# A decoder layer with a sparse mixture of experts on one core: expert weights in 2 MB transfers, and a front end split around its row transposes

## The chip, the cores and the metric

The kernel is one program on 1 core of one Trainium2 chip. Its time is the device time of one execution, in microseconds (us), launch to end. Five engines work side by side: TensorE (PE in the profile; PEld is its weight load), VectorE (DVE), ScalarE (ACT), GpSimd (POOL) and SyncE (SP), which here issues nearly all DMA transfers. Sixteen DMA engines share every transfer. "MB" of an expert transfer below is 1,048,576 bytes; the GB/s of the profile are 1e9 bytes per second.

## What is computed

One layer of a decoder for 256 prompt rows and 8 x 4 sample rows, with all weights and caches in float32. A modulation (`silu(c) @ w_ada + b_ada`), an RMS norm, and one wide projection `w_in` feed a sparse attention (compressed, selected and window branch) and a gated recurrence; their merged result goes through `w_out`. Then comes the mixture of experts, in which most of the time is spent:

```python
def moe_ffn(h, w_router, b_router, w_up, b_up, w_down, b_down):
    logits = (xt @ w_router + b_router).astype(jnp.float32)
    top_v, top_i = lax.top_k(logits, TOP_K)          # 4 of 32
    wts = jax.nn.softmax(top_v, axis=-1)
    ...
    for e in range(N_EXPERTS):
        z = xt @ w_up[e] + b_up[e]                   # 1024 x 2048
        gate = jnp.minimum(z[:, :D_EXPERT], SWIGLU_LIMIT)
        up = jnp.clip(z[:, D_EXPERT:], -SWIGLU_LIMIT, SWIGLU_LIMIT)
        act = (up + 1.0) * gate * jax.nn.sigmoid(SWIGLU_ALPHA * gate)
        out = out + gate_dense[:, e:e + 1] * (act @ w_down[e] + b_down[e])   # 1024 x 1024
```

The compressed branch needs a convolution of the cached keys and values (`compress`: blocks of 32 rows, stride 16, against `cmp_w1`).

## The kernel before

All tiles lie in one SBUF array, `arena`; PSUM is eight banks. Each engine has its own hand-written program, and semaphores join them; nothing is scheduled by a planner in the parts that follow, except the order of some steps in the middle of the program, which is not touched.

**Front end.** TensorE first transposes the gathered cache rows (L764). Then it runs `convolve(0)` (L786: 32 taps by two halves, 64 matrix products of 504 columns, two records each in the trace), then for each of three row tiles `rows_to_hT(n)` (L753: transposes of the input rows) followed by `modulation(n)` (L798: one slab of `w_ada` against the conditioning vectors), then `position_terms` (L774, L778), `modulation` 3 to 5, four transposes (L815), `convolve(1)`, and the compressed keys and values (L821, L824).

**Slabs.** `w_ada` (12 slabs) and the main part of `w_in` (7 slabs) come in slabs of 2 MB (the last one smaller) with runs of 2 KB, in the order of `SLABS`: six of `w_ada`, one of `w_in`, then turns of both. Three buffers hold them; SP issues slab i (L570) as soon as slab i-3 is used (`slab_used`). A slab of `w_in` costs TensorE the products at L1002, L1003 and L1008. Behind slab 9 SP issues `state_win`, the cached rows of the window, for six of the eight samples in one transfer of 3 MB (L594), once both convolutions are done (`pre_ps`). `window_keys` reads it after the slabs.

**Experts.** Tokens are packed into chunks of 64 slots; 34 chunks serve the 32 experts, so two experts have two chunks. An expert's weights come in 12 pieces of 1 MB: eight of `w_up` (128 rows each, a run of 8 KB in a partition) and four of `w_down` (256 rows, two neighbouring rows in a partition, also 8 KB). The pieces go round a ring of 21 places. For each chunk TensorE adds the bias (L1320), multiplies pieces q = 0 to 7 (L1328, eight records a piece), dispatches the next chunk's tokens (L1299), transposes the activations (L1343, L1305), and multiplies pieces q = 8 to 11 (L1358, eight records a piece). It waits for a piece by `ld_piece`, and counts it used by `piece_used`. SP refills a place when the piece in it is used for the last time: for an expert with two chunks that is in the second one, since the wait (L710 for the last, L705 for the others) counts from `until`, the number of that expert's last chunk. Before the first chunk SP fills the ring in steps: 8 pieces once the merged rows are there (`mT`), 4 after the output projection (`out_ps`), 8 after `y1`, `h2` and the router (`lg_ps`), the last one after `wdiag`.

**End.** GpSimd scatters each chunk's result to `slots` in DRAM (L2302, L2303). After the last one SP reads them back in two transfers of 2 MB with runs of 16 KB (L719), and TensorE sums them (L1382).

Of the kernel before, what the change touches and what calls it, by code (L numbers as in the profile page):

```python
# [243 lines left out]
ORDER = (2, 0, 1)  # L244
PIECES = 12 * E


def build(nc, A, O):

    with ExitStack() as ctx:  # L250
# [166 lines left out]
        def ftake(n, *shape):  # L417
# [83 lines left out]

        up_pairs = up.rearrange("p (m t v) -> p m v t", m=2, v=2)
        in_chunk = [view(low + 12 * NCHUNK * i, 12 * NCHUNK, 12, NCHUNK) for i in range(2)]
# [11 lines left out]
        assert ring_at - routed >= 2 * D and ring_at + 7 * 2 * D <= wo_at and CONSTS["chunk0"][0] + NCHUNK <= x_at - 2 * D  # L515
        places = ([ring_at + 2 * D * i for i in range(7)] + [x_at - 2 * D] + [ring_at + 2 * D * i for i in range(7, 16)]
                  + [x_at, spare, spare + 2 * D, routed])
        ring = [view(a, 2 * D) for a in places]
        R_ = len(ring)
# [29 lines left out]
        def _(sp):  # L549
# [33 lines left out]
            for i in range(3, len(SLABS)):  # L583
                load_slab(i)
                if i == 6:
                    sp.wait_ge(S("pair_ps"), 32)
                    for w, name in enumerate(("norm_mix_post", "norm_ffn_pre", "norm_ffn_post")):
                        for j in range(4):
                            src = A[name][0].rearrange("(n j c) -> j n c", j=4, c=P)[j]
                            sp.dma_start(wn[32 * j:32 * j + 32, 2 * w:2 * w + 2], src.unsqueeze(0).broadcast_to([32, 2, P])  # L590
                                         ).then_inc(S("ld_wn"), 16)
                if i == 9:
                    sp.wait_ge(S("pre_ps"), 2)
                    sp.dma_start(arena[:, gates_at:gates_at + 6 * 1024].rearrange("p (b c) -> p b c", b=6),  # L594
                                 A["state_win"][0, 0:6].rearrange("b (p s) k g d -> p b (s k g d)", s=4)).then_inc(S("ld_win"), 16)
            sp.wait_ge(S("mod_v"), 12)
# [87 lines left out]
            for n in range(R_):  # L684
                if n == 8:
                    sp.wait_ge(S("out_ps"), 5)
                if n == 12:
                    sp.wait_ge(S("y1"), 3)
                    sp.dma_start(xd[0:TP].rearrange("(i p) d -> p i d", p=P), x[:, 0:2]).then_inc(S("st_state"), 16)
                    sp.dma_start(xd[TP:TP + NS], x[0:NS, 2]).then_inc(S("st_state"), 16)  # L690
                    sp.wait_ge(S("h2"), 3)
                    for r in range(4):
                        sp.dma_start(bias[32 * r:32 * r + E], A["b_up"][0][:, 512 * r:512 * r + 512]).then_inc(S("ld_bias"), 16)
                    sp.wait_ge(S("lg_ps"), 3)
                if n == 17:
                    sp.wait_ge(S("st_state"), 64)
                if n == R_ - 1:
                    after(sp, "wdiag")
                load_piece(n)
            after(sp, "tab")  # L700
            for n in range(R_, PIECES):
                e, q = (n - R_) // 12, (n - R_) % 12
# [28 lines left out]
        def _(pe):  # L731
# [48 lines left out]

            def convolve(g):
                for s in range(32):
# [4 lines left out]
                last.then_inc(S("pre_ps"), 1)  # L787

# [27 lines left out]
            last.then_inc(S("modT_ps"), 1)  # L816
            convolve(1)
            pe.wait_ge(S("gelu"), 4)
# [86 lines left out]
            def window_keys(b):  # L905
                pe.wait_ge(S("ld_win" if b < 6 else "ld_win2"), 16)
                bank = to_ring("win", b)
# [395 lines left out]
            def chunk_T():  # L1303
                for k in range(4):
                    last = nc.tensor.transpose(banks[2][:, P * k:P * k + P], xr[:, P * k:P * k + P], ident)  # L1305
                last.then_inc(S("xcT_ps"), 1)
# [7 lines left out]
            for e in range(E):  # L1314
                before = pe.value_load(tab[0:1, E + e:E + e + 1], min_val=0, max_val=CMAX)
                upto = pe.value_load(tab[0:1, e:e + 1], min_val=1, max_val=CMAX)
                with pe.Fori(before, upto) as c:
# [5 lines left out]
                    for q in range(8):  # L1323
                        n = 12 * e + q
                        pe.wait_ge(S(f"ld_piece{n % R_}"), 16 * (n // R_) + 16)
                        for part in range(2):
                            for s in range(2):
                                last = mm(banks[part][SLOT * s:SLOT * s + SLOT, :], xcT[:, q],  # L1328
                                          ring[n % R_][:, D * part + 512 * s:D * part + 512 * s + 512], start=False, stop=q == 7)
                        last.then_inc(S("piece_used"), 1)  # L1330
# [11 lines left out]
                    for k in range(4):  # L1342
                        last = nc.tensor.transpose(banks[(3, 6)[k // 2]][:, P * (k % 2):P * (k % 2) + P], up_pairs[:, k // 2, k % 2], ident)  # L1343
                        if k % 2:
                            last.then_inc(S("aT_ps"), 1)
# [3 lines left out]
                    for q in range(8, 12):  # L1349
                        n = 12 * e + q  # L1350
                        if q < 10:
                            pe.wait_ge(S("aT"), c * 2 + (q - 7))
                        pe.wait_ge(S(f"ld_piece{n % R_}"), 16 * (n // R_) + 16)
                        for v in range(2):
                            f = 2 * (q - 8) + v
                            lhs = aT[:, P * (f % 4) + SLOT * (f // 4):P * (f % 4) + SLOT * (f // 4) + SLOT]
                            for s in range(2):
                                last = mm(banks[4][SLOT * s:SLOT * s + SLOT, :], lhs,  # L1358
                                          ring[n % R_][:, D * v + 512 * s:D * v + 512 * s + 512], start=f == 0, stop=f == 7)
                        last.then_inc(S("piece_used"), 1)  # L1360
# [972 lines left out]
```

## Time and profile before

| | us |
|---|---|
| median of 3 runs | 1562.64 (1561.87 to 1564.94) |
| the profiled execution's own time | 1568.19 |
| its span, first to last instruction | 1565.0 |
| PE busy in the span | 1431.4 (91%) |
| DVE busy | 362.5 (23%) |
| ACT busy | 296.9 (19%) |
| POOL busy | 81.4 (5%) |
| data moved | 513.19 MB, mean 328 GB/s |

A share of busy time says little here, since the stages have different limits: the span has a front end (0 to about 265 us), a middle (to about 515 us), the ring's filling with the router (to about 580 us), the experts (to about 1531 us) and an end. Which wait ends last must be read in each. In a timeline row the bracket at the end is the engine's idle time just before and what ended it.

### The profile page before, as it was taken

How to read it: one execution, taken by the hardware profiler on the slowest of the kernel's cores; microseconds unless marked ns; L12 is line 12 of the kernel's file. 1: busy time of each engine (PE TensorE's matmuls, PEld its weight loads, DVE VectorE, ACT ScalarE, POOL GpSimd, SP SyncE). 2: the span in 40 equal slices, each digit the busy share in tenths (PEclk: the TensorE clock that was granted, in tenths of full speed). 3: DMA queues.
4: the chain of work that ended last, by engine and by line, in shares of the span. 5: the costliest groups of instructions: out<-in, count | busy, mean ns of one | idle time of the engine just before them, and what ended most of it. 6: DMA issues, size and time to landing. Idle time of an engine off the chain costs nothing.

```text
span 1565.0 us, 21038 instructions
## 1 busy us (share of the span) xinstructions
PE 1431.4 (91%) x8523; PEld 632.6 (40%) x8523; DVE 362.5 (23%) x833; ACT 296.9 (19%) x568; POOL 81.4 (5%) x108
## 2 busy tenths in 40 slices
PE   4999999979998979999999999999998998899895
PEld 4564455456766443333333333333332322232231
DVE  5220012347752351111111111121211111111123
ACT  4110003455420221101111111111110110111011
POOL 2000001300000000000000000000000000000000
PEclk9899999989899969999999999999999999999998
DMA  9791775414177589979999999999999999999994
GB/s 277 239 334 54 271 255 183 130 43 153 50 199 261 217 358 402 419 293 421 420 420 420 420 420 419 421 421 419 421 420 420 420 420 420 420 420 420 420 403 173
DMA packets 119925, 513.19 MB, mean 328 GB/s; under 512 B 12945, under 2 KB 42025, under 8 KB 68194
## 3 DMA queue, kind: packets, MB, share of 16 engines
q1 hardware_dynamic: 113090, 489.91, 79.3%
q0 software_dynamic: 6752, 22.06, 4.1%
q8 instruction: 66, 1.08, 0.3%
q14 instruction: 17, 0.14, 0.0%
HBM read 501.06 MB, written 19.22 MB: 332 GB/s over the span
## 4 chain that ended last, share of the span: by engine, by line
PE 60%; DMA 29%; DVE 5%; ACT 2%; SPq 1%; issue 1%; POOL 0%; DVEq 0%; POOLq 0%; ACTq 0%
DMA arena<-in_w_up 23%; PE bank L1328 20%; PE bank L1358 9%; PE bank L1170 4%; PE bank L786 4%; PE bank L1002 3%; PE bank L1003 3%; DMA arena<-in_w_in 2%; PE bank L1263 2%; DMA arena<-in_cache_cmp,arena 2%; PE bank L1320 1%; PE bank L1249 1%; PE bank L1251 1%; PE bank L1343 1%; DMA arena<-in_w_ada 1%
## 5 line engine op out<-in xcount | busy, mean ns | idle before, releaser
L1328 PE MATMUL bank<-arena 128*64 128x512 f32 x2176 | 493.8, 599 | 33.2 <-DMA arena<-in_w_up 33.0
L1328 PEld LDWEIGHTS bank<-arena 128*64 128x64 f32 x2176 | 145.0, 136 | 351.9 <-issue 265.4
L1358 PE MATMUL bank<-arena 128*64 128x512 f32 x1088 | 241.0, 595 | 0.0
L2228 DVE TENSOR_SCALAR arena<-bank,arena 128x1 uint32<-128x1 f32 x34 | 7.4, 219 | 593.4 <-PE bank L1336 593.4
L1358 PEld LDWEIGHTS bank<-arena 128*64 128x64 f32 x1088 | 75.0, 136 | 141.8 <-issue 136.1
L1700 ACT ACTIVATE arena<-arena 128x512 f32<-128x512 f32 x34 | 21.4, 630 | 528.3 <-DVE arena L2231 528.3
L1299 PE MATMUL bank<-arena 128*64 128x512 f32 (+1 forms) x420 | 103.9, 613 | 2.9 <-DVE arena L2189 2.9
L2302 POOL DMA_DIRECT2D slots<-arena x34 | 18.7, 549 | 1169.9 <-ACT arena L1707 1169.9
L1170 PE MATMUL bank<-arena 128*128 128x288 f32 x256 | 70.1, 421 | 1.9 <-DMA arena<-in_w_in 0.8
L1002 PE MATMUL bank<-arena 128*128 128x512 f32 (+1 forms) x112 | 58.8, 606 | 10.1 <-DMA arena<-in_w_in 7.0
L2231 DVE TENSOR_SCALAR arena<-bank 128x512 f32<-128x512 f32 x34 | 23.5, 692 | 185.4 <-PE bank L1328 185.4
L1707 ACT COPY arena<-bank 128x512 f32<-128x512 f32 x34 | 19.9, 585 | 221.4 <-PE bank L1358 221.4
L786 PE MATMUL bank<-arena 64*128 64x504 f32 x256 | 56.1, 596 | 1.7 <-DVE arena L1767 1.7
L1299 PEld LDWEIGHTS bank<-arena 128*64 128x64 f32 (+1 forms) x420 | 27.0, 136 | 72.5 <-issue 69.4
L1003 PE MATMUL bank<-arena 128*128 128x512 f32 (+1 forms) x112 | 56.3, 585 | 0.0
L1170 PEld LDWEIGHTS bank<-arena 128*128 128x128 f32 x256 | 48.2, 197 | 18.3 <-issue 4.4
L1700 ACT ACT_TABLE_LOAD x34 | 43.6, 1283 | 0.6
L786 PEld LDWEIGHTS bank<-arena 64*128 64x128 f32 x256 | 27.9, 191 | 28.8 <-issue 28.8
L1320 PE MATMUL bank<-arena 32*64 32x512 f32 x272 | 37.9, 627 | 0.7 <-ACT arena L1691 0.7
L764 PE MATMUL bank<-arena 128*128 128x128 f32 x128 | 21.4, 329 | 16.1 <-DMA arena<-in_cache_cmp,arena 14.6
L2303 POOL DMA_INDIRECT slots<-arena x34 | 35.4, 1042 | 10.3 <-issue 10.3
L1002 PEld LDWEIGHTS bank<-arena 128*128 128x128 f32 x112 | 21.7, 200 | 32.2 <-issue 22.3
(414 smaller groups left out, 1261.0 us busy)
## 6 DMA issues: line engine op xcount, KB each, us to landing
arena<-in_w_up SPq DMA_DIRECT2D x256, 1024.0 KB, 26.9
arena<-in_w_down SPq DMA_DIRECT2D x128, 1024.0 KB, 26.6
arena<-in_w_ada SPq DMA_DIRECT2D x12, 2048.0 KB, 11.6
arena<-in_w_in SPq DMA_DIRECT2D x6, 2048.0 KB, 13.3
arena<-in_w_in SPq DMA_DIRECT2D x16, 512.0 KB, 3.9
arena<-in_w_out SPq DMA_DIRECT2D x1, 4096.0 KB, 16.0
arena<-slots SPq DMA_DIRECT2D x2, 2048.0 KB, 10.1
out<-in_state_win SPq DMA_DIRECT2D x1, 4064.0 KB
```

The source lines that it names most:

```text
L786: last = mm(banks[2 * g + v][:, 0:NB * NCMP], w1[half, s], src, start=s == 0, stop=s == 31)
L1002: mm(b0[:, 0:w], hT[:, k, 0:P], columns(k, 0, w), start=first, stop=final)
L1003: mm(b1[:, 0:w], hT[:, k, P:2 * P], columns(k, 0, w), start=first, stop=final)
L1170: last = mm(banks[7][:, 0:TP + NS], gate_piece[j % 2][:, k], hT[:, k], start=k == 0, stop=k == KD - 1)
L1263: last = mm(banks[(6, 2)[i] + n][:], mT[:, k, P * i:P * i + P], wo[k][:, 512 * n:512 * n + 512], start=k == 0, stop=k == KD - 1)
L1299: last = mm(banks[5][SLOT * s:SLOT * s + SLOT, :], oneslot[0:ROWS[i], i], h2r[0:ROWS[i], i, 512 * s:512 * s + 512], start=i == 0, stop=i == 2)
L1320: mm(banks[r // 2][SLOT * (r % 2):SLOT * (r % 2) + SLOT, :], ident[32 * r:32 * r + E, 32 * r + e:32 * r + e + 1].broadcast_to([E, SLOT]), ...
L1328: last = mm(banks[part][SLOT * s:SLOT * s + SLOT, :], xcT[:, q], ring[n % R_][:, D * part + 512 * s:D * part + 512 * s + 512], start=False ...
L1358: last = mm(banks[4][SLOT * s:SLOT * s + SLOT, :], lhs, ring[n % R_][:, D * v + 512 * s:D * v + 512 * s + 512], start=f == 0, stop=f == 7)
L1700: fn(sg, gt, ACT.Sigmoid, scale=1.702).then_inc(S("sig"), 1)
L2231: V.tensor_scalar(gt, banks[0][:], 7.0, None, ALU.min).then_inc(S("gate"), 1)
L2303: pool.indirect_dma_start(out=results, out_offset=bass.IndirectOffsetOnAxis(ap=rowu[:, 0:1], axis=0), in_=yc, in_offset=None, bounds_check ...
```

## The change

Four things are changed, and nothing is computed otherwise.

1. The first convolution is run in two halves, taps 0 to 15 ahead of the row transposes and the first three modulations, taps 16 to 31 behind them.
2. `state_win` of six samples is loaded in three transfers of 1 MB, behind slabs 9, 11 and 13.
3. The expert pieces are 2 MB with runs of 16 KB: six to an expert (four of `w_up`, of 256 rows, two rows in a partition; two of `w_down`, of 512 rows, four in a partition). The ring has 10 places of 2 MB, 20 MB in all against 21 MB; it gives up the place `routed`. TensorE waits once for every two of its old pieces, and SP for `piece_used` in steps of two.
4. Since rows lie in other partitions, the transposes read with a stride: of `xr` every second column (L1305), of `up` every fourth (L1343) where it was every second.

```diff
-PIECES = 12 * E
+PIECES = 6 * E
...
-        up_pairs = up.rearrange("p (m t v) -> p m v t", m=2, v=2)
+        up_fours = up.rearrange("p (t v) -> p v t", v=4)
+        xr_pairs = xr.rearrange("p (m t v) -> p m v t", m=2, v=2)
...
-        places = ([ring_at + 2 * D * i for i in range(7)] + [x_at - 2 * D] + [ring_at + 2 * D * i for i in range(7, 16)]
-                  + [x_at, spare, spare + 2 * D, routed])
-        ring = [view(a, 2 * D) for a in places]
+        places = [ring_at + 4 * D * i for i in range(8)] + [x_at - 2 * D, spare]
+        ring = [view(a, 4 * D) for a in places]
...
-                if i == 9:
+                if i in (9, 11, 13):
+                    b = i - 9
                     sp.wait_ge(S("pre_ps"), 2)
...
-                e, q = n // 12, n % 12
-                if q < 8:
-                    src = w_up[e, P * q:P * q + P]
-                    dst = ring[n % R_]
+                e, q = n // 6, n % 6
+                if q < 4:
+                    src = w_up[e, 2 * P * q:2 * P * (q + 1)].rearrange("(p k) n -> p k n", k=2)
+                    dst = ring[n % R_].rearrange("p (k n) -> p k n", k=2)
                 else:
-                    src = w_down[e, 2 * P * (q - 8):2 * P * (q - 7)].rearrange("(p k) n -> p k n", k=2)
-                    dst = ring[n % R_].rearrange("p (k n) -> p k n", k=2)
+                    src = w_down[e, 4 * P * (q - 4):4 * P * (q - 3)].rearrange("(p k) n -> p k n", k=4)
+                    dst = ring[n % R_].rearrange("p (k n) -> p k n", k=4)
...
-                if n == 8:
+                if n == 3:
                     sp.wait_ge(S("out_ps"), 5)
-                if n == 12:
+                if n == 5:
                     sp.wait_ge(S("y1"), 3)
...
-                if n == 17:
+                if n == 8:
                     sp.wait_ge(S("st_state"), 64)
...
-                sp.wait_ge(S("piece_used"), until * 12 + (q + 1))
+                sp.wait_ge(S("piece_used"), until * 12 + 2 * (q + 1))
...
-            convolve(0)
+            convolve(0, 0, 16)
             after(pe, "peT")
             for n in range(3):
                 rows_to_hT(n)
                 modulation(n)
+            convolve(0, 16, 32)
             position_terms()
...
                     for q in range(8):
-                        n = 12 * e + q
-                        pe.wait_ge(S(f"ld_piece{n % R_}"), 16 * (n // R_) + 16)
+                        n = 6 * e + q // 2
+                        if q % 2 == 0:
+                            pe.wait_ge(S(f"ld_piece{n % R_}"), 16 * (n // R_) + 16)
```

How the instructions stand, at three places. TensorE in the front end, before (x64 and so on count instructions of the program, 32 of them at L798 being one slab):

```order
L764 MATMUL bank<-arena 128x128 x128
L786 MATMUL bank<-arena 128x504 x64
L753 MATMUL bank<-arena 128x128 x8
L798 MATMUL bank<-arena 32x128 x32
L753 MATMUL bank<-arena 128x128 x8
L798 MATMUL bank<-arena 32x128 x32
L753 MATMUL bank<-arena 128x32 x8
L798 MATMUL bank<-arena 32x128 x32
L774 MATMUL bank<-arena 1x128 x64
```

The same place in the changed kernel, whose lines are one to three numbers higher:

```order
L765 MATMUL bank<-arena 128x128 x128
L787 MATMUL bank<-arena 128x504 x32
L754 MATMUL bank<-arena 128x128 x8
L800 MATMUL bank<-arena 32x128 x32
L754 MATMUL bank<-arena 128x128 x8
L800 MATMUL bank<-arena 32x128 x32
L754 MATMUL bank<-arena 128x32 x8
L800 MATMUL bank<-arena 32x128 x32
L787 MATMUL bank<-arena 128x504 x32
L775 MATMUL bank<-arena 1x128 x64
```

Half of the convolution has moved behind the three slabs; what follows is in the old order.

SP at slabs 9 to 13, before:

```order
L570 DMA arena<-in_w_ada 128x8x512 [waits slab_used]
L594 DMA arena<-in_state_win 128x6x1024 [waits pre_ps]
L570 DMA arena<-in_w_in 128x8x512 [waits slab_used]
L570 DMA arena<-in_w_ada 128x8x512 [waits slab_used]
L570 DMA arena<-in_w_in 128x8x512 [waits slab_used]
```

In the changed kernel:

```order
L570 DMA arena<-in_w_ada 128x8x512 [waits slab_used]
L595 DMA arena<-in_state_win 128x2x1024 [waits pre_ps]
L570 DMA arena<-in_w_in 128x8x512 [waits slab_used]
L570 DMA arena<-in_w_ada 128x8x512 [waits slab_used]
L595 DMA arena<-in_state_win 128x2x1024 [waits pre_ps]
L570 DMA arena<-in_w_in 128x8x512 [waits slab_used]
```

The 3 MB ahead of slab 10 have become 1 MB there, 1 MB ahead of slab 12 and 1 MB ahead of slab 14.

SP at the filling of the ring, before (`dve_step` is here the wait for `wdiag`, then for `tab`):

```order
L681 DMA arena<-in_w_up 128x2048 [waits mT]
L681 DMA arena<-in_w_up 128x2048 x7
L681 DMA arena<-in_w_down 128x2048 [waits out_ps]
L681 DMA arena<-in_w_down 128x2048 x3
L689 DMA xd<-arena 128x2x1024 [waits y1]
...
L681 DMA arena<-in_w_up 128x2048 [waits lg_ps]
L681 DMA arena<-in_w_up 128x2048 x4
L681 DMA arena<-in_w_up 128x2048 [waits st_state]
L681 DMA arena<-in_w_up 128x2048 x2
L681 DMA arena<-in_w_down 128x2048 [waits dve_step]
```

In the changed kernel:

```order
L682 DMA arena<-in_w_up 128x4096 [waits mT]
L682 DMA arena<-in_w_up 128x4096 x2
L682 DMA arena<-in_w_up 128x4096 [waits out_ps]
L682 DMA arena<-in_w_down 128x4096
L690 DMA xd<-arena 128x2x1024 [waits y1]
...
L682 DMA arena<-in_w_down 128x4096 [waits lg_ps]
L682 DMA arena<-in_w_up 128x4096 x2
L682 DMA arena<-in_w_up 128x4096 [waits st_state]
L682 DMA arena<-in_w_up 128x4096 [waits dve_step]
```

What stood as 8, 4, 8 and 1 MB behind the waits for `mT`, `out_ps`, `lg_ps` and `wdiag` is now 6, 4, 8 and 2 MB.

## Rows read from the trace of the kernel before

**Rows 1.** The page: the span, and its DMA rate in 40 slices.
```profile
span 1565.0 us, 21038 instructions
GB/s 277 239 334 54 271 255 183 130 43 153 50 199 261 217 358 402 419 293 421 420 420 420 420 420 419 421 421 419 421 420 420 420 420 420 420 420 420 420 403 173
```

**Rows 2.** Chain of waits, last part: start us, us, what.
```profile
1491.16 26.36 DMA arena<-in_w_up
...
1523.60 7.04 PE bank L1358 x32
...
1537.78 12.32 DMA arena<-slots
```

**Rows 3.** Windows of the expert phase: us, busy per engine, PEclk, DMA share, GB/s.
```profile
684.80:692.60 7.80, 7.80 (x42) 2.34 (x40) 0.00 (x0) 1.87 (x2) 1.59 (x2) 1.00 0.00 0
692.60:1517.50 824.90, 786.11 (x4000) 262.99 (x3996) 114.05 (x234) 106.62 (x145) 46.09 (x58) 1.00 1.01 420
```

**Rows 4.** Timeline of TensorE, last expert and final sums.
```profile
1515.08 1.94 PE L1328 MATMUL bank<-arena 128*64 128x512 f32 x8 [0.55 <-DMA arena<-in_w_up]
1517.57 1.94 PE L1328 MATMUL bank<-arena 128*64 128x512 f32 x8 [0.55 <-DMA arena<-in_w_up]
...
1522.42 0.74 PE L1343 MATMUL bank<-arena 128*128 128x128 f32 x4 [0.20 <-DVE arena L2238]
1523.00 0.60 PE L1305 MATMUL bank<-arena 128*128 128x128 f32 x4
```

**Rows 5.** The page: DMA issues, KB each, median us to landing.
```profile
arena<-in_w_up SPq DMA_DIRECT2D x256, 1024.0 KB, 26.9
...
arena<-in_w_ada SPq DMA_DIRECT2D x12, 2048.0 KB, 11.6
...
arena<-slots SPq DMA_DIRECT2D x2, 2048.0 KB, 10.1
```

**Rows 6.** Timeline of SP: the two reads of the slots.
```profile
1537.31 0.90 SPq L719 DMA_DIRECT2D arena<-slots  x2
```

**Rows 7.** DMA packets of 1541 to 1549 us, by queue: packets, MB, share.
```profile
q1 hardware_dynamic: 226, 3.34, 97.6%
```

**Rows 8.** Timeline of TensorE, front end.
```profile
45.54 28.75 PE L786 MATMUL bank<-arena 64*128 64x504 f32 x128 [1.69 <-DVE arena L1767]
...
90.88 4.00 PE L798 MATMUL bank<-arena 128*32 128x128 f32 x128
97.63 1.96 PE L798 MATMUL bank<-arena 128*32 128x128 f32 x64 [2.75 <-DMA arena<-in_w_ada]
```

**Rows 9.** Timeline of TensorE around the wait for slab 10.
```profile
151.07 1.13 PE L1002 MATMUL bank<-arena 128*128 128x512 f32 x2
...
165.03 1.96 PE L1008 MATMUL bank<-arena 128*32 128x128 f32 x64
...
172.11 2.08 PE L1002 MATMUL bank<-arena 128*128 128x512 f32 x2 [3.38 <-DMA arena<-in_w_in]
...
189.01 1.96 PE L1008 MATMUL bank<-arena 128*32 128x128 f32 x64
```

**Rows 10.** Windows: busy per engine, then PEclk, DMA share, GB/s.
```profile
168.70:172.10 3.40, 0.04 (x4) 0.00 (x0) 0.29 (x1) 0.00 (x0) 0.00 (x0) 0.87 1.05 385
172.10:178.70 6.60, 6.59 (x9) 2.82 (x10) 0.00 (x0) 0.00 (x0) 0.00 (x0) 0.55 1.05 387
```

**Rows 11.** Timeline of SP: slabs 0 to 2, 3 to 5, and 9.
```profile
34.89 13.55 SPq L570 DMA_DIRECT2D arena<-in_w_ada  x3
...
77.27 5.79 SPq L570 DMA_DIRECT2D arena<-in_w_ada  x3
...
149.45 0.37 SPq L570 DMA_DIRECT2D arena<-in_w_ada  x1
```

**Rows 12.** Timeline of SP: pieces ahead of and behind the full ring.
```profile
662.24 33.21 SPq L681 DMA_DIRECT2D arena<-in_w_down  x4
```

**Rows 13.** Timeline of SP from 690 us: the pieces behind it.
```profile
691.68 2.04 SPq L681 DMA_DIRECT2D arena<-in_w_down  x2
```

More of the change, by code:

```diff
@@ L591, in _ @@
                                          ).then_inc(S("ld_wn"), 16)
-                if i == 9:
+                if i in (9, 11, 13):
+                    b = i - 9
                     sp.wait_ge(S("pre_ps"), 2)
-                    sp.dma_start(arena[:, gates_at:gates_at + 6 * 1024].rearrange("p (b c) -> p b c", b=6),
-                                 A["state_win"][0, 0:6].rearrange("b (p s) k g d -> p b (s k g d)", s=4)).then_inc(S("ld_win"), 16)
+                    sp.dma_start(arena[:, gates_at + 1024 * b:gates_at + 1024 * (b + 2)].rearrange("p (b c) -> p b c", b=2),
+                                 A["state_win"][0, b:b + 2].rearrange("b (p s) k g d -> p b (s k g d)", s=4)).then_inc(S("ld_win"), 16)
             sp.wait_ge(S("mod_v"), 12)
@@ L701, in _ @@
             for n in range(R_, PIECES):
-                e, q = (n - R_) // 12, (n - R_) % 12
+                e, q = (n - R_) // 6, (n - R_) % 6
                 if q == 0:
                     until = sp.value_load(tab[0:1, 2 * E + e:2 * E + e + 1], min_val=0, max_val=CMAX - 1)
-                sp.wait_ge(S("piece_used"), until * 12 + (q + 1))
+                sp.wait_ge(S("piece_used"), until * 12 + 2 * (q + 1))
                 load_piece(n)
@@ L779, in position_terms, with convolve @@
                 last.then_inc(S("pconst_ps"), 1)
-            def convolve(g):
-                for s in range(32):
+            def convolve(g, first, past):
+                for s in range(first, past):
                     for v in range(2):
@@ L786, in convolve @@
                         last = mm(banks[2 * g + v][:, 0:NB * NCMP], w1[half, s], src, start=s == 0, stop=s == 31)
-                last.then_inc(S("pre_ps"), 1)
+                if past == 32:
+                    last.then_inc(S("pre_ps"), 1)
             def modulation(i):
@@ L816, in _ @@
             last.then_inc(S("modT_ps"), 1)
-            convolve(1)
+            convolve(1, 0, 32)
             pe.wait_ge(S("gelu"), 4)
@@ L905, in window_keys @@
             def window_keys(b):
-                pe.wait_ge(S("ld_win" if b < 6 else "ld_win2"), 16)
+                if b < 6:
+                    pe.wait_ge(S("ld_win"), 48)
+                else:
+                    pe.wait_ge(S("ld_win2"), 16)
                 bank = to_ring("win", b)
@@ L1304, in chunk_T @@
                 for k in range(4):
-                    last = nc.tensor.transpose(banks[2][:, P * k:P * k + P], xr[:, P * k:P * k + P], ident)
+                    last = nc.tensor.transpose(banks[2][:, P * k:P * k + P], xr_pairs[:, k // 2, k % 2], ident)
                 last.then_inc(S("xcT_ps"), 1)
@@ L1323, in _ @@
                     for q in range(8):
-                        n = 12 * e + q
-                        pe.wait_ge(S(f"ld_piece{n % R_}"), 16 * (n // R_) + 16)
+                        n = 6 * e + q // 2
+                        if q % 2 == 0:
+                            pe.wait_ge(S(f"ld_piece{n % R_}"), 16 * (n // R_) + 16)
                         for part in range(2):
                             for s in range(2):
-                                last = mm(banks[part][SLOT * s:SLOT * s + SLOT, :], xcT[:, q],
-                                          ring[n % R_][:, D * part + 512 * s:D * part + 512 * s + 512], start=False, stop=q == 7)
+                                at = 2 * D * (q % 2) + D * part + 512 * s
+                                last = mm(banks[part][SLOT * s:SLOT * s + SLOT, :], xcT[:, q], ring[n % R_][:, at:at + 512],
+                                          start=False, stop=q == 7)
                         last.then_inc(S("piece_used"), 1)
@@ L1342, in _ @@
                     for k in range(4):
-                        last = nc.tensor.transpose(banks[(3, 6)[k // 2]][:, P * (k % 2):P * (k % 2) + P], up_pairs[:, k // 2, k % 2], ident)
+                        last = nc.tensor.transpose(banks[(3, 6)[k // 2]][:, P * (k % 2):P * (k % 2) + P], up_fours[:, k], ident)
                         if k % 2:
@@ L1349, in _ @@
                     for q in range(8, 12):
-                        n = 12 * e + q
+                        n = 6 * e + q // 2
                         if q < 10:
                             pe.wait_ge(S("aT"), c * 2 + (q - 7))
-                        pe.wait_ge(S(f"ld_piece{n % R_}"), 16 * (n // R_) + 16)
+                        if q % 2 == 0:
+                            pe.wait_ge(S(f"ld_piece{n % R_}"), 16 * (n // R_) + 16)
                         for v in range(2):
@@ L1357, in _ @@
                             for s in range(2):
-                                last = mm(banks[4][SLOT * s:SLOT * s + SLOT, :], lhs,
-                                          ring[n % R_][:, D * v + 512 * s:D * v + 512 * s + 512], start=f == 0, stop=f == 7)
+                                at = 2 * D * (q % 2) + D * v + 512 * s
+                                last = mm(banks[4][SLOT * s:SLOT * s + SLOT, :], lhs, ring[n % R_][:, at:at + 512],
+                                          start=f == 0, stop=f == 7)
                         last.then_inc(S("piece_used"), 1)
```

## The prediction, made before the changed kernel was run

> **What bounds the kernel now.** I read the page first, for the stages, then the chain of waits, then windows and timelines where the chain leaves TensorE. From slice 19 on the DMA rate is 420 GB/s in every slice [rows 1]. The chain's last part is a wait for a `w_up` piece until 1517.5 us, then the last expert's work, then the read of the slots [rows 2]. From 692.6 to 1517.5 us the DMA share is full at 420 GB/s [rows 3]: here the stream of pieces sets the end, and TensorE is fed piece by piece, 2.49 us apart (1515.08, 1517.57) [rows 4]. A piece lands 26.9 us after its issue [rows 5], so the queue holds ten others: the issue itself limits nothing.
>
> The stream stands still once before: DMA does nothing from 684.8 to 692.6 us [rows 3]. Fifty-seven pieces are there, 36 of them used and 21 in the ring; the fourth expert has two chunks, so no place comes free until its second chunk starts. Piece 56 was issued at 662.24, piece 57 at 691.68 [rows 12, 13]. This splits the program: until 691.68 TensorE sets the time, behind it DMA does. What the front end gains moves the restart with it; what the filling of the ring gains or loses is swallowed, as long as the ring gets full again.
>
> **Front end.** Convolution halves: the three slabs of `modulation` 0 to 2 are used some 14 us sooner, so slabs 3 to 5, now issued from 77.27 [rows 11], can land sooner by as much. TensorE's work is the same, and it loses the wait of 2.75 us ahead of `modulation(5)` [rows 8]. Their cover: slab 2 is issued by 48.4 [rows 11], lands at about 60 (11.6 us is the median [rows 5]), and is wanted near 66 (half of L786's 28.75 us from 45.54 on [rows 8], then 6 us of transposes and slabs). If it came late, the convolution's second half would not hide it; I see no such thing. Gain 2.75 us, bounds 0 and 2.75.
>
> `state_win` in three: slab 10 has 2 MB of slab 9, 3 MB of `state_win` and its own 2 MB ahead of it from 149.45 on [rows 11], and TensorE waits 3.38 us for it until 172.11 [rows 9]. Two of these MB (2.1e6 bytes at 385 GB/s [rows 10]) are 5.4 us, so it lands at 166.7, ahead of the 168.7 at which it is wanted. The wait goes. Behind it the granted clock was 0.55 for 6.6 us, from 1.00 on, after 3.4 us in which TensorE did nothing [rows 10]: near the lower of its two levels, 1.2 and 2.4 GHz. The slab took 189.01 - 172.11 = 16.90 us to L1008, the one before 165.03 - 151.07 = 13.96 [rows 9]: 2.94 us more. Without the idle stretch I expect this to go too, 3.38 + 2.94 = 6.32 us. What is late next: slabs 12 and 14, which now have 1 MB more ahead of them. The queue of slab 12 is then what slab 10's was, landing 17.2 us after slab 11's issue; TensorE wants it after 13.96 + 1.9 + 2 x 1.8 = 19.4 us. The margin is 2 us each time. Front end together: **9.1 us less** (bounds 2.75 and 9.1).
>
> The middle takes this over whole: its loads are issued on TensorE's counts. The filling delivers 6, 4, 8 and 2 MB where it was 8, 4, 8 and 1; pieces are wanted only from 582 us on, and the ring gets full at about 686 instead of 684.8, well ahead of the restart. So this costs nothing; with no full ring behind it, it would cost 2 MB, 5 us.
>
> **The restart.** The smaller ring holds 56 MB instead of 57 when it is full, and its first place is free only when two old pieces of the second chunk are used, one later: 1.75 us (L1328 and L1358 run at 7.04/4 a piece [rows 2]). The megabyte missing costs one step, 2.49 - 0.04. Together **4.2 us more**. At the second two-chunk expert (near 970 us) the same could happen; there 20 us of pieces stood in the queue, and 5 are lost: no stall.
>
> **The stream.** From there to the last `w_up` piece are 324 MB, 162 transfers, of which I count 161 steps. A step of 2 MB is now 4.97 us. The two reads of the slots have the new form, 2 MB in runs of 16 KB: issued 0.45 apart from 1537.31 [rows 6], median 10.1 [rows 5], the second 12.3 [rows 2], so the first 7.9; they landed 12.3 - 7.9 + 0.45 = 4.88 apart. By share, 97.6% of 16 engines for 8 us is 124.9 us for 204 packets of 16 KB and 22 of a few bytes [rows 7], 0.612 us each, 4.90 a step. I take 4.88: 161 x 0.09 = **14.5 us less**. The bounds: 4.90 gives 11.3; from above, 16 KB no better than 8 KB gives 0. The other loads of the phase (GpSimd's scatter, instruction fetches) stay.
>
> The Trainium skill gives an engine a fixed cost of some 3 cycles a packet on top of 32 bytes a cycle ("DMA: Bandwidth & Descriptors", Why small descriptors are slow). By that, doubling the run saves 0.6% of the step, an estimate of 4.7 us instead of 14.5. The rows above show 1.8%, and they decide; no run here has shown it beside matmuls.
>
> **The tail.** With piece 6 and 7 landing as one, TensorE has two old pieces to do behind it: **1.75 us more**. The last `w_down` transfer lands two steps later, 9.8 us, and is wanted 11 us later (3.5 for the two pieces, 4.1 from there to L1358, 3.5 for its first half): no wait. The strided transposes: L1343 (stride 2) takes 0.74, L1305 (stride 1) 0.60 [rows 4]. L1305 gets stride 2, 0.14; stride 4 for L1343 has no row, from 0 to again 0.14 x 2. They count in the four chunks before the restart and the last one: 5 x 0.2 = **1.0 us more** (0.7 to 2.1); elsewhere the wait for pieces, some 3 us an expert, hides them.
>
> **Sum.** -9.1 + 4.2 - 14.5 + 1.75 + 1.0 = -16.6 us. Against the profiled execution (1568.19, span 1565.0 [rows 1] and 3.2 around it) that is 1551.6 and a span of 1548.4. The median of the runs is 5.6 us below the profiled one; I carry this over: 1562.64 - 16.6 = **1546.0 us**.
>
> **Rivals.**
> - *The packets gain little.* The runs may be cut again, or the overhead may lie in something that 16 KB does not halve. For: only two transfers speak for 4.88, at a time when TensorE did little. Against: the spacing and the share agree to 0.02. At half the gain 1553.3, at none 1560.5. The Trainium skill's packet rule, above, would put this rival at 1555.8 by its estimate.
> - *The slabs are late after all.* 2 us of margin at slabs 12 and 14 is small; if one is late the clock falls again, 2.94 us and the wait. For: three steps of this kind come in a row. Against: the rate is steady, 385 and 387 GB/s in two stretches [rows 10]. It gives back about 6 us: 1552.
> - *Larger packets slow the stream* (the other side). Eight streams of one engine's partitions now stride 16 KB in DRAM, and 128 rows start together. If banks collide, the step grows. At the 385 GB/s of the slabs [rows 10] a step is 5.45 us, 161 x 0.48 = 77 more: 1637. It decides from a step of 5.00 us on, where -2.1 becomes +3.1. [...] Against: the slots were read at a pitch of 16 KB, too.
> - *The restart comes later*, or a second full ring: 2 to 6 us, 1548 to 1552.
>
> **Chances.** The forecast, 1541 to 1551: 0.66. Packets gain little: 0.13, of which 0.04 at nothing, near 1560. Slabs late: 0.10. Later restart: 0.05. Slower stream: 0.06. A measurement of this kernel can tell 0.2%, 3.1 us. Faster by more: 0.90; within: 0.04; slower: 0.06. The range of 8 in 10 takes in the forecast, the late slabs, the later restart and half the packet gain: 1541 to 1556.
>
> **What would show it.** Right: no row of TensorE waiting for `w_ada` before `convolve(1)` nor for `w_in` at slab 10; the one for the last slabs (near 225 now) stays. L1002 at 0.87 us a pair throughout. SP's gap at the full ring, from about 680, restart near 684.4 (693.4 - 9.1). Windows behind it at 427 to 429 GB/s. The last expert's L1328 rows in groups of 16 records, 4.88 apart. Wrong: packets of 8 KB or less in the DMA counts; DMA idle near 970; a rate at 420 or below; waits at slabs 12 or 14.

## The result, and the profile after

| | before | after |
|---|---|---|
| median of 4 runs, us | 1562.61 (1561.87 to 1564.94) | 1551.81 (1547.74 to 1554.82) |
| ratio | | 0.992 [0.9893, 0.9946] |
| profiled execution, own time and span, us | 1568.19, 1565.0 | 1551.22, 1549.2 |

The forecast was 1546.0 (1541 to 1556). The measured 1551.8 lies 5.8 us above it and inside the range. The change gains 10.8 us in this comparison, where the sum said 16.6. Between the two profiled executions it gains 17.0. Both differences are samples from a spread, as the experiments show: with about 30 runs of the kernel before beside it, the changed kernel is 15.0 us faster. In the changed kernel's source the lines lie a little lower (L798 is L800, L1002 L1008, L1328 L1336, L1343 L1351, L1305 L1311, L1358 L1368, L681 L682; its L1305 is the dispatch, L1299 before).

The page of the changed kernel, span and DMA rate in 40 slices (before: [rows 1]):

```profile
span 1549.2 us, 20633 instructions
GB/s 278 346 234 88 308 279 156 72 57 150 55 224 227 189 356 428 427 289 428 426 427 427 427 428 425 427 427 428 428 425 427 426 427 426 427 428 425 427 390 162
```

From slice 19 on it is 425 to 428 GB/s where it was 419 to 421, up to the last two slices, in which the stream ends. The end of the chain of waits has kept its shape ([rows 2]): a `w_up` transfer, the last expert, the slots. Start us, us, what:

```profile
1455.28 44.63 DMA arena<-in_w_up
1507.77 7.04 PE bank L1368 x32
1521.91 12.39 DMA arena<-slots
```

Windows of the full ring and of the stream, with busy time per engine (PE, PEld, DVE, ACT, POOL), granted clock, DMA share and GB/s (before: [rows 3]):

```profile
677.10:684.80 7.70, 7.70 (x42) 2.35 (x40) 0.00 (x0) 1.87 (x2) 1.59 (x2) 1.00 0.09 34
692.60:1499.90 807.30, 774.08 (x3944) 265.04 (x3940) 113.59 (x232) 106.60 (x145) 46.08 (x58) 1.00 1.01 427
```

The ring still gets full once (DMA share 0.09 ahead of 684.8). SP's timeline of the changed kernel shows the issue behind it at 684.85, where it was 691.68 [rows 13]:

```profile
639.02 14.94 SPq L682 DMA_DIRECT2D arena<-in_w_up  x4
684.85 3.76 SPq L682 DMA_DIRECT2D arena<-in_w_down  x2
```

Timeline of TensorE in the last expert of the changed kernel (before: [rows 4]). L1336 is fed in groups of 16 records now (split here by another line's records), and the last 16 start at 1499.96, 0.05 us behind the landing of their transfer:

```profile
1497.47 1.94 PE L1336 MATMUL bank<-arena 128*64 128x512 f32 x8
1499.96 3.66 PE L1336 MATMUL bank<-arena 128*64 128x512 f32 x16 [0.55 <-DMA arena<-in_w_up]
1503.44 2.89 PE L1305 MATMUL bank<-arena 128*64 128x512 f32 x12
1506.53 0.75 PE L1351 MATMUL bank<-arena 128*128 128x128 f32 x4 [0.19 <-DVE arena L2248]
1507.12 0.65 PE L1311 MATMUL bank<-arena 128*128 128x128 f32 x4
```

Timeline of TensorE in the front end of the changed kernel (before: [rows 8, 9]):

```profile
67.31 13.79 PE L787 MATMUL bank<-arena 64*128 64x504 f32 x64
...
89.34 5.46 PE L800 MATMUL bank<-arena 128*32 128x128 f32 x192
...
162.07 1.93 PE L800 MATMUL bank<-arena 128*32 128x128 f32 x64
163.93 1.13 PE L1008 MATMUL bank<-arena 128*128 128x512 f32 x2
...
223.60 1.47 PE L1008 MATMUL bank<-arena 128*128 128x512 f32 x2 [3.98 <-DMA arena<-in_w_in]
```

`modulation` 3 to 5 run in one piece of 192 records without the wait for `w_ada`, and slab 10's first product follows with no bracket. Nor has any product of slab 12 or 14 a bracket. The wait for slab 17 (3.62 us before, 3.98 in the last row here) stands.

**Marks.** Cutting the profiled executions at the same events shows where the time went. "Last slabs" is the first product of L862 (before), behind slab 17; only the smaller slab 18 follows it. "First chunk" is the first product of the bias, L1320 before. "58 MB" is the landing of the 58th megabyte of expert weights, the first behind the full ring before (in the changed kernel it lands in one transfer with the 57th), "last w_up" the landing of the last `w_up` transfer.

| us | before | before, again | after | after, again | after, third |
|---|---|---|---|---|---|
| last slabs | 254.31 | 249.35 | 242.72 | 243.02 | 243.92 |
| first expert transfer issued | 515.16 | 510.33 | 506.76 | 507.23 | 507.85 |
| first chunk (bias) | 580.84 | 575.60 | 572.04 | 572.71 | 573.13 |
| 58 MB landed | 697.51 | 692.42 | 692.62 | 693.64 | 694.25 |
| last w_up landed | 1517.52 | 1512.40 | 1499.91 | 1500.77 | 1500.77 |
| TensorE's last expert product | 1530.62 | 1525.50 | 1514.79 | 1515.65 | 1515.65 |
| span | 1565.0 | 1561.4 | 1549.2 | 1551.5 | 1549.9 |

### The profile page after: what moved, and what is told of

The parts are those of the page before. It is cut to its first block, busy times and chain, and to the rows that moved or that the text cites. A ratio compares the mean times of both kernels' runs of the same rounds, so it can differ in the third digit from the quotient of the medians.

```text
span 1549.2 us, 20633 instructions
## 1 busy us (share of the span) xinstructions
PE 1428.2 (92%) x8523; PEld 637.8 (41%) x8523; DVE 362.6 (23%) x833; ACT 296.8 (19%) x568; POOL 81.4 (5%) x108
## 4 chain that ended last, share of the span: by engine, by line
PE 64%; DMA 24%; DVE 7%; ACT 2%; issue 1%; SPq 1%; POOL 0%; DVEq 0%; POOLq 0%; ACTq 0%
PE bank L1336 20%; DMA arena<-in_w_up 20%; PE bank L1368 12%; PE bank L787 4%; PE bank L1176 3%; PE bank L1008 3%; PE bank L1009 3%; PE bank L1269 2%; DMA arena<-in_cache_cmp,arena 2%; PE bank L1326 1%; PE bank L1351 1%; DVE arena L2248 1%; DVE arena L2245 1%; DVE arena L2241 1%; PE bank L800 1%
## 5 line engine op out<-in xcount | busy, mean ns | idle before, releaser
L1336 PE MATMUL bank<-arena 128*64 128x512 f32 x2176 | 491.3, 599 | 27.7 <-DMA arena<-in_w_up 27.5
L1336 PEld LDWEIGHTS bank<-arena 128*64 128x64 f32 x2176 | 147.6, 137 | 339.4 <-issue 282.4
L1368 PE MATMUL bank<-arena 128*64 128x512 f32 x1088 | 241.0, 595 | 0.0
L1368 PEld LDWEIGHTS bank<-arena 128*64 128x64 f32 x1088 | 74.9, 136 | 140.2 <-issue 136.1
L1305 PE MATMUL bank<-arena 128*64 128x512 f32 (+1 forms) x420 | 103.5, 611 | 3.0 <-DVE arena L2199 3.0
L1176 PE MATMUL bank<-arena 128*128 128x288 f32 x256 | 74.8, 442 | 2.4 <-DMA arena<-in_w_in 1.3
L1008 PE MATMUL bank<-arena 128*128 128x512 f32 (+1 forms) x112 | 56.1, 580 | 6.2 <-DMA arena<-in_w_in 4.0
L1176 PEld LDWEIGHTS bank<-arena 128*128 128x128 f32 x256 | 50.5, 206 | 20.0 <-issue 3.5
L1305 PEld LDWEIGHTS bank<-arena 128*64 128x64 f32 (+1 forms) x420 | 27.0, 136 | 72.5 <-issue 69.4
L1009 PE MATMUL bank<-arena 128*128 128x512 f32 (+1 forms) x112 | 55.0, 573 | 0.0
L765 PE MATMUL bank<-arena 128*128 128x128 f32 x128 | 20.1, 319 | 17.1 <-DMA arena<-in_cache_cmp,arena 16.6
L1351 PEld LDWEIGHTS bank<-arena 128*128 128x128 f32 x136 | 19.0, 209 | 36.5 <-DVE arena L2248 36.5
## 6 DMA issues: line engine op xcount, KB each, us to landing
arena<-in_state_win SPq DMA_DIRECT2D x4, 1024.0 KB, 10.8
```

Of the source, the lines that this page charges most:

```text
L1008: mm(b0[:, 0:w], hT[:, k, 0:P], columns(k, 0, w), start=first, stop=final)
L1009: mm(b1[:, 0:w], hT[:, k, P:2 * P], columns(k, 0, w), start=first, stop=final)
L1176: last = mm(banks[7][:, 0:TP + NS], gate_piece[j % 2][:, k], hT[:, k], start=k == 0, stop=k == KD - 1)
L1305: last = mm(banks[5][SLOT * s:SLOT * s + SLOT, :], oneslot[0:ROWS[i], i], h2r[0:ROWS[i], i, 512 * s:512 * s + 512], start=i == 0, stop=i == 2)
L1368: last = mm(banks[4][SLOT * s:SLOT * s + SLOT, :], lhs, ring[n % R_][:, at:at + 512], start=f == 0, stop=f == 7)
```

## The experiments

Each kernel ran beside the kernel before on one chip; a ratio is to that. The pooled medians of before were 1566.65 (29 runs, 1561.8 to 1572.9), 1566.87 (31 runs, 1560.2 to 1570.7) and 1567.03 (11 runs, 1562.4 to 1569.8). The profiled 1568.19 and the 1562.6 of the first comparison both lie inside that spread, and the profiled executions of the kernels below lie on either side of their medians, within 3 us. So nothing here shows that a profiled execution is longer as a rule, and the 5.6 us that the prediction took from one to the other look like chance.

**Before, unchanged.** No edit.

> The kernel before, unchanged, profiled once more. Theory A (the profiled execution of before was a slow one by chance): this one lies near the median, about 1562.6, and its trace is some 5 us shorter than 1565.0, either in the front and middle, where granted clock and waits vary, or in the stream of pieces behind the restart. Theory B (a profiled execution of this kernel is always some 5 us longer than the others): 1568 again, with a span near 1565.

Measured: 1565.89, ratio 0.9993 [0.9974, 1.0013], span 1561.4. The trace is 5.0 us shorter than the first one of before at the last slabs, and 5.1 at TensorE's last expert product; the end takes 1.5 us longer, so the span is 3.6 shorter. The profiled execution of before was a slow one, as theory A had it; the median that it names, 1562.6, was itself low. Timeline of TensorE at slab 10, and the window behind its wait:

```profile
170.12 1.13 PE L1002 MATMUL bank<-arena 128*128 128x512 f32 x2 [2.36 <-DMA arena<-in_w_in]
```

```profile
170.10:176.70 6.60, 6.58 (x16) 2.98 (x17) 0.00 (x0) 0.00 (x0) 0.00 (x0) 1.00 1.05 387
```

The wait is there, 2.36 us instead of 3.38, but the granted clock behind it is 1.00, the upper level, where it was 0.55 [rows 10]. In a further old front end (the experts-only kernel below) the same wait was 2.15 us, and the first products behind it took 1.87 and 1.92 us a pair instead of 1.02; with the convolution halves alone it was 2.69 us, and the first pair behind it took 1.13 us, as in a slab with no wait. So the clock falls behind this wait in some executions only, in two of these four, and the wait's length does not decide it.

**Front end only.** Edits 1 and 2 of the change on the kernel before.

> The convolution in halves and state_win in three loads, expert pieces of 1 MB as before. Theory A (parts add up, the middle hands most of it on): TensorE's first wait for a piece count (restart) comes 8 to 9 us sooner, and so does the end: 1562.6 - 8.5 = 1554. Theory B (the middle swallows half of what the front gives, through clock and load waits that fall elsewhere): restart only 4 to 5 us sooner, 1558.

Measured: 1560.85, ratio 0.9961 [0.9945, 0.9977], -5.8 us. That is between the two theories, nearer to B. Last slabs at 243.75, 5.6 sooner than in "before, again"; at the first chunk 2.1 are left, since this execution's middle is one of the long ones (see below).

**Experts only.** Edits 3 and 4 on the kernel before.

> Pieces of 2 MB in runs of 16 KB and a ring of 10 places, front end as before. Theory A: restart 4.1 us later in landed bytes, stream 12.7 us shorter than 820.0 from there to the last w_up piece, tail 1.75 longer: 6.8 less, 1556. Theory B (the median of the whole change, 10.8 less, is mostly front end): 1 to 3 us less, 1560.

Measured: 1560.49, ratio 0.9961 [0.9944, 0.9977], -6.2 us. Theory A said 6.8 less. The two parts make -12.0, the whole -15.0 (next run); with intervals of some 2.6 us either way on each part and 5 on the whole they agree. From 58 MB to the last `w_up` it takes 807.4 us.

**After, again.** No edit of the changed kernel.

> The changed kernel, unchanged, once more beside the parts. Both theories: a median near 1551.8 with a spread of some 7 us. Theory A: the spread lies in the front and middle (granted clock below 1.00 at varying places), the stream from the restart to the last w_up piece takes 807 us again within 1 us. Theory B: the stream itself varies by several us.

Measured: 1551.67 (1548.57 to 1556.3), ratio 0.9902 [0.987, 0.9933], -15.0 us. The stream takes 807.1 us by the marks above, as in theory A.

**Convolution halves only**, and **`state_win` in three only**: edit 1 alone, edit 2 alone.

```diff
-            convolve(0)
+            convolve(0, 0, 16)
...
+            convolve(0, 16, 32)
```

> The convolution in halves alone; state_win in one load, pieces of 1 MB. Theory A (each front part takes away its own wait and nothing else): no wait ahead of the sixth modulation (2.4 to 3.1 us before), the wait for slab 10 stays at 2.2 to 3.4 us; 1566.7 - 2.8 = 1563.9. Theory B (the split only shifts load against work, so that slab 10 comes later by as much): nothing measured.

```diff
-                if i == 9:
+                if i in (9, 11, 13):
```

The transfer's source and the wait for it (`ld_win`) are changed with it.

> state_win in three loads alone. Theory A: no wait for slab 10, where 2.2 to 3.4 us were, and no wait at slabs 12 and 14; the clock behind slab 10 stays at 1.00; in executions where it fell behind the wait this gives up to 3 us more. 1566.7 - 3.2 = 1563.5. Theory B (the clock fall is part of the wait every time): 1560.4.

Measured: halves 1562.94, ratio 0.9973 [0.9958, 0.9987], -3.9 us; `state_win` 1563.8, ratio 0.9979 [0.9962, 0.9996], -3.1 us. With `state_win` alone, slab 10 has no wait, and the one ahead of `modulation(5)` stays; this is TensorE's row there:

```profile
95.86 1.96 PE L799 MATMUL bank<-arena 128*32 128x128 f32 x64 [2.92 <-DMA arena<-in_w_ada]
```

With the halves alone it is the other way round: none there, 2.69 us at slab 10. Each edit removes its own wait. The last slabs are passed 4.4 and 3.5 us sooner than in "before, again". These two make 7.9 where both edits together had 5.6, and the medians -7.0 where they had -5.8: single executions differ by as much, in the clock above all.

**2 MB transfers with runs of 8 KB.** The changed kernel, with rows laid out as before, and the transposes with their old strides; of the expert part only transfer size and ring stay changed.

```diff
-                    src = w_up[e, 2 * P * q:2 * P * (q + 1)].rearrange("(p k) n -> p k n", k=2)
+                    src = w_up[e, 2 * P * q:2 * P * (q + 1)].rearrange("(k p) n -> p k n", p=P)
...
-                    src = w_down[e, 4 * P * (q - 4):4 * P * (q - 3)].rearrange("(p k) n -> p k n", k=4)
-                    dst = ring[n % R_].rearrange("p (k n) -> p k n", k=4)
+                    src = w_down[e, 4 * P * (q - 4):4 * P * (q - 3)].rearrange("(a p k) n -> p a (k n)", a=2, k=2)
+                    dst = ring[n % R_].rearrange("p (a n) -> p a n", a=2)
```

> The changed kernel with its 2 MB transfers made of runs of 8 KB (rows and transposes as before, two blocks of 1 MB side by side in a place). Theory A (the run's length carries the stream's gain): 322 MB from the restart on take 820 us as before, the end is 12.7 us later than the changed kernel's: 1564.5. Theory B (the size of the transfer carries it, fewer issues and completion counts): about 807 us and 1552.

Measured: 1564.46, ratio 0.9984 [0.9969, 0.9998]. It is 12.8 us slower than the changed kernel (theory A said 12.7), and the stream is back at the old pace, 819.8 us from 58 MB to the last `w_up`. DMA counts of 900 to 1400 us, of this kernel and then of the changed one: all packets, then queue, packets, MB, share of 16 engines:

```profile
DMA packets 28870, 210.22 MB, mean 420 GB/s; under 512 B 2885, under 2 KB 2885, under 8 KB 3565
...
q1 hardware_dynamic: 26866, 207.14, 99.6%
```

```profile
DMA packets 16443, 213.42 MB, mean 427 GB/s; under 512 B 2911, under 2 KB 2911, under 8 KB 3583
...
q1 hardware_dynamic: 14447, 210.36, 99.0%
```

The queue is full in both and the transfer has the same size; the one with about half the packets moves 1.6% more in them. Transfer size alone brings nothing. In this kernel L1350 and L1310 (this kernel's L1351 and L1311) take 0.74 and 0.60; with strides 4 and 2 it is 0.75 and 0.65, in the rows above.

**A ring of nine places.** The changed kernel with one place less.

```diff
         places = [ring_at + 4 * D * i for i in range(8)] + [x_at - 2 * D, spare]
+        places = places[:7] + places[8:]
...
-                if n == 8:
+                if n == 7:
```

> The changed kernel with 9 places of 2 MB instead of 10. Theory A (behind the full ring the end is set by what the ring holds at the restart): the restart's issue stays where it is against the first chunk, 2 MB fewer are there, so the end is 4.9 us later, 1556.6; the full ring stands still 5 us longer. At the second expert with two chunks no stall. Theory B (the ring's size is hidden, since the queue is never empty): no change. Theory C (the second expert with two chunks stalls as well): 8 us or more.

Measured: 1558.98, ratio 0.9944 [0.9922, 0.9966]. From the first chunk to the 58th megabyte it takes 125.6 us: 120.6 to 121.1 with ten places, 116.7 with the old ring of 21 MB. The stream behind it takes 807 us, and the rate from 940 to 1010 us is 426 GB/s, so the second expert with two chunks stalls nothing, and theory C falls. The marks show 4.4 to 5.0 us more, about the one step of 4.9 of theory A for the 2 MB missing when the ring is full. The medians lie 7.3 us apart, with an interval of some 3.4 either way on this kernel's; the spans lie 2.4 to 4.7 apart, and this execution has one of the short middles (see below).

**Slabs in turn to the end.** The changed kernel, with `w_ada` 10, `w_in` 5, `w_ada` 11, `w_in` 6, to remove the wait for slab 17; the compressed scores and their softmax move behind `w_in` 6.

```diff
-SLABS += [("a", 10), ("a", 11), ("w", NZ - 2), ("w", NZ - 1)]
+SLABS += [("a", 10), ("w", NZ - 2), ("a", 11), ("w", NZ - 1)]
...
-                if n == NZ - 2:
+                if n == NZ - 1:
                     compressed_scores()
```

ScalarE's and VectorE's parts of the softmax are moved in the same way.

> The changed kernel with one more edit, after the same pattern: the last four slabs come as w_ada 10, w_in 5, w_ada 11, w_in 6 instead of w_ada 10, 11, w_in 5, 6, and the work on the compressed scores hangs behind w_in 6 instead of w_in 5. In the changed kernel TensorE waits 3.98 us for w_in 5 until 223.60. Now this slab lands one transfer of 2 MB sooner, 5.4 us, at 218.2, and is wanted 1.9 us sooner (one slab of w_ada less ahead of it), near 217.7: the wait shrinks to about 0.5 us. Theory A (the wait is on the path, and nothing else is late there): the clock's fall behind it goes too in most executions, so the counts of own scores start 3.5 to 5 us sooner, and the end comes 3 to 5 us sooner than the changed kernel's: ratio to the kernel before 0.987 to 0.988. Theory B (the slab's work had covered another chain: the softmax of the compressed scores on VectorE and ScalarE now stands behind w_in 6 with only the own sums to hide it): TensorE waits there instead for 2 to 5 us, and the time is that of the changed kernel or up to 2 us more, ratio 0.990 to 0.992.

**After, third.** No edit; on the same chip as the last one.

> The changed kernel once more, beside the one with the other slab order, on the same chip. Expected: the ratio of before, 0.990 to 0.991, and in its trace 807 us between the landing of the 58th and the 380th megabyte, 4.0 us more between the first chunk and the 58th megabyte than with 1 MB pieces, and 14.9 us from the last w_up transfer to TensorE's last expert matmul. The stretch between the last slab and the first expert transfer has so far been 261 or 264 us in executions of either kernel; it should be one of the two again. Theory A of the middle (the granted clock of 320 to 350 us decides): if it is 261, the granted clock of the 30 us that begin 81 us behind the last slab is 0.94 or more, and 0.89 if it is 264. Theory B: the clock there does not go with it.

Measured: in turn 1550.04 (1546.6 to 1552.73), ratio 0.9893 [0.987, 0.9916]; after, third 1552.69, ratio 0.9915 [0.9895, 0.9935]. TensorE at `w_in` 5, with the slabs in turn and then in the third run of the changed kernel:

```profile
216.16 1.94 PE L800 MATMUL bank<-arena 128*32 128x128 f32 x64
218.02 1.13 PE L1008 MATMUL bank<-arena 128*128 128x512 f32 x2
```

```profile
224.39 2.08 PE L1008 MATMUL bank<-arena 128*128 128x512 f32 x2 [4.06 <-DMA arena<-in_w_in]
```

The wait of 4.06 us is gone whole, and the clock is 1.00 behind it (0.88 in the other, mean of the 18 us that this slab takes). L873, the first product after all slabs and own scores, starts at 253.34 instead of 258.45, 5.1 us sooner; the first chunk at 570.29 instead of 573.13, 2.8 us sooner; the spans differ by 2.1, the medians by 2.65. The softmax is no obstacle (a wait of 0.61 us ahead of L873), so theory B falls; A is right on the wait and too high on the end, since the middle gave 2.3 us back. The intervals of the two ratios overlap: this version is probably some 2 us faster than the changed kernel, which these runs don't separate.

**The middle.** From the last slabs to the first expert transfer it takes 261 us in three executions (before, before again, ring of nine) and 263.8 to 264.8 in the eight others of the old slab order. Experts-only, with the old front end, is at 263.8, and the ring of nine, with the new one, at 261.0, so neither front end fixes it; whether the new one makes the longer value more frequent stays open. The expectation above tied it to the clock of 81 to 111 us behind the last slabs; the first two runs of the changed kernel had 0.89 there, but the third has 0.95 and yet takes 263.9. The timelines of TensorE part later. The same eight products of a gate, 150 us behind the last slabs, with the ring of nine (L1177) and then in the third run (L1176, same code):

```profile
393.21 2.11 PE L1177 MATMUL bank<-arena 128*128 128x288 f32 x8
```

```profile
393.07 1.93 PE L1139 MATMUL bank<-arena 128*128 128x16 f32 x16 [0.77 <-DVE arena L2049]
...
395.32 3.44 PE L1176 MATMUL bank<-arena 128*128 128x288 f32 x8
```

A short fall of the clock meets heavy products in one execution and light ones in the other, 1.3 us apart here, and the wait for VectorE (0.77 us) stands ahead of it in the slower one. An earlier gate, too, took 4.05 us against 2.76, but at the next pair of gates, 142 us behind the last slabs, the two stand within 0.2 us of each other again. Windows of 137 to 143 and 150 to 156 us behind the last slabs, with the ring of nine and then in the third run:

```profile
379.80:385.80 6.00, 4.67 (x23) 2.71 (x23) 5.90 (x13) 4.83 (x14) 0.00 (x0) 0.72 0.15 45
392.80:398.80 6.00, 6.00 (x36) 4.43 (x36) 5.22 (x12) 3.00 (x10) 0.00 (x0) 1.00 0.01 3
```

```profile
380.90:386.90 6.00, 3.82 (x26) 2.48 (x27) 5.89 (x11) 5.16 (x15) 0.00 (x0) 1.00 0.15 45
393.90:399.90 6.00, 6.00 (x30) 4.03 (x29) 4.81 (x10) 1.99 (x7) 0.00 (x0) 0.72 0.01 3
```

The clock falls in the first window where the middle is short, among waits for other engines, and in the second where it is long, under full work. All three short executions have the first pattern and seven of the eight long ones the second; experts-only has the first and is long all the same, with a clock of 0.84 in the 30 us that begin 81 us behind the last slabs. That the clock starts this, and isn't a follower, was not tested.

## Why the prediction was right, and where not

**Waits in the front end: right.** 2.75 us ahead of `modulation(5)` and 3.38 at slab 10 are gone, each by its own edit; slabs 12 and 14 come in time, as the margin of 2 us said: TensorE waits at neither, so that rival falls.

**The clock behind slab 10: a term that was mis-sized.** "I expect this to go too, 3.38 + 2.94" took one execution's fall for the rule. In "before, again" wait and clock together cost 2.36 us, and the changed front end is 5.4 to 6.6 us faster there (last slabs), not 9.1; against the first profile of before it is 11.6. The step should have counted 2.94 with a chance, which makes 6.1 to 9.1.

**"The middle takes this over whole": right only within 3 us.** The middle's own length takes one of two values, 3 us apart. Between the first two profiles 11.6 us became 8.4 at the first expert transfer. The medians, over many executions, give the front end 5.8 us.

**The restart: right.** Predicted 4.2 and 0.8 for the transposes ahead of it; from the first chunk to the 58th megabyte it was 116.7 us and is 120.6 to 121.1, 3.9 to 4.4 more. In the first profiles the issue comes 2.0 us later behind the first chunk (112.8 instead of 110.8, predicted 1.75) and its landing 1.9 more (predicted 2.45). The ring of nine repeats the missing step at 4.4 to 5.0. No second full ring near 970 us: the rate there is 425 GB/s or more.

**The stream: right in kind, 1.9 us too high.** "161 x 0.09 = 14.5 us less." The 161 steps took 819.9 us with runs of 8 KB and 807.3 with 16 KB (5.09 and 5.01 each, the other traffic of the phase included): 12.6 less, 0.078 a step. The spacing of the two slots reads, 4.88, was one sample; the share of the engines, 4.90, was the lower bound of the gain with 11.3, and the result lies between. Between 900 and 1400 us packets of 16 KB took a median of 613 ns in the changed kernel, those of 8 KB 312 ns before: two old ones take 11 ns more than one new, 1.8%. A step has 128 new packets, 8 for each of the 16 engines, so this alone makes some 0.09 us a step, near the 0.078 measured. The Trainium skill ("DMA: Bandwidth & Descriptors", Why small descriptors are slow) gives a packet some 3 cycles of fixed cost, by which an estimate of 4.7 us was to be had; the runs show 12.6, and the measurement decides. The rival of banks in conflict at a pitch of 16 KB falls, since the rate rose. One reading was too wide: the 420 GB/s "in every slice" from 19 on are 419 to 421, and the last two slices, 403 and 173, lie outside; the stream's window stops before them, so the sum does not use them.

**The tail: right.** 13.10 us from the last `w_up` to TensorE's last expert product became 14.88, 1.78 more (predicted 1.75 and 0.2).

**The transposes: too high.** 0.2 us a chunk was to be paid, since the 0.14 between L1343 and L1305 was read as the price of the stride; stride 4 against stride 2 costs 0.01 and stride 2 against 1 costs 0.05 for four of them, so most of the 0.14 is something else, which no run here names. Five times 0.06 is 0.3 us, not 1.0.

**The sum and the level.** With the sizes measured, -5.8 (front end, by its medians), +4.2 (restart), -12.6 (stream) and +1.8 (tail) make -12.4, with the transposes' 0.3 inside the restart and the tail, and the two parts' medians -12.0; the whole came at -15.0 and -14.3 beside the larger samples, and at -10.8 in the first comparison. These agree within their intervals; no trace shows a stretch that only the whole kernel wins. The predicted -16.6 was too large a gain, by 1.6 us against the whole's -15.0 and by 4.2 against the sum of the sizes. The level was the larger miss: "The median of the runs is 5.6 us below the profiled one; I carry this over" put the sum on a median of three runs, 1562.64, where some 30 runs have 1566.8. From there -16.6 would have given 1550.2; the changed kernel's three medians are 1551.8, 1551.7 and 1552.7. So the 5.8 us between forecast and result are some 4.2 of level and some 1.6 of gain. That the result stayed in the range is in part luck: it lies just outside the 1541 to 1551 to which the prediction gave 0.66, and the rivals that it placed near there (late slabs 1552, a later restart up to 1552, half the packet gain 1553.3) did not come true.

## What to carry to other kernels

When a stream of DMA sets the end and its queue never runs empty, look at the length of its runs and not at the size of its transfers, and count what larger pieces cost at both ends, at a full ring and behind the last piece (here 6 of 12.6 us). What the clock did behind one wait in one profile is a chance and not a price: profile the unchanged kernel twice before it enters a sum. The level on which a sum is set needs enough runs for the difference that it is to show; three runs of this kernel were 4 us off.

## What the runs showed of the hardware

- Runs of 16 KB instead of 8 KB raised a stream with a full queue from 420 to 427 GB/s, beside matmuls; 2 MB instead of 1 MB a transfer, with runs of 8 KB, left it at 420.
- Behind the wait for the same slab, TensorE's granted clock was 1.00 after 2.36 us idle in one execution and 0.55 after 3.38 in another of the same code; in two further kernels with that code it fell after 2.15 us and not after 2.69.
- Four transposes that read every fourth column took 0.75 us, every second 0.74 (L1343) or 0.65 (L1311), neighbouring ones 0.60 (L1305).
- The same program's runs spread over 1560 to 1573 us; its two profiled executions took 1568.2 and 1563.7.
